# Order of small loads and head tiles, features-first queries and keys, scores in pairs, in a fused two-block transformer kernel

## What is computed

```python
mod = silu(c) @ w_ada + b_ada                     # 2048 x 12288, six vectors
h = rmsnorm(x, norm1_g) * (1 + sc1) + sh1
proj = h @ w_in                                   # 2048 x 5456
# stick-breaking: q_sb, k_sb, v_sb, 8 heads of 128; z = q k^T
# sparse attention: 8 heads of 128, one k and v, indexer of 16 heads of 64, top 64 keys
# then w_out, and a gated FFN with a causal conv of width 3
for l in range(2):                                # block 2, two layers
    proj = rms_norm(x) @ w_in[l]                  # 2048 x 6726
    # A: 6 heads of 128 with a forget gate, cum_logf = cumsum(log_sigmoid(a_f + b_forget))
    # B: latent attention, q = rms_norm(b_cq) @ w_uq (512 x 6*(128+64)), kv from w_ukv
    s = q_nope @ k_nope^T + q_rope @ k_rope^T     # 6 heads, 128 + 64 features, k_rope shared
    # C: differential attention, 4 heads, two score sets of 64 features each
    w = softmax(q1 @ k1^T) - lam * softmax(q2 @ k2^T)
    x = x + mixed @ w_out[l]
```

## Time and profile before

| | us |
|---|---|
| median of 3 runs (lowest, highest) | 2160.98 (2159.06, 2162.43) |
| profiled execution, own time | 2168.37 |
| its span | 2166.6 |
| PE busy | 2086.6 (96%) |
| PE weight loads busy | 1864.6 (86%) |
| DVE busy | 1405.5 (65%) |
| ACT busy | 1012.0 (47%) |
| POOL busy | 129.5 (6%) |
| chain that ended last, share of PE | 87% |

### The profile page before, as it was taken

One profiled execution on the slowest core, in us unless ns is written; L12 is line 12 of the kernel. 1 busy time (PEld: TensorE's weight loads), 2 busy tenths in 40 slices (PEclk: granted clock), 3 DMA queues, 4 the chain that ended last, 5 costly groups with the idle time before them and its releaser, 6 DMA issues.

```text
span 2166.6 us, 34209 instructions
## 1 busy us (share of the span) xinstructions
PE 2086.6 (96%) x13672; PEld 1864.6 (86%) x13672; DVE 1405.5 (65%) x2152; ACT 1012.0 (47%) x1498; POOL 129.5 (6%) x113
## 2 busy tenths in 40 slices
PE   4989999998999999999999999999999999999997
PEld 1668888787999999998888899998978999999876
DVE  2348998886667567666576576455566655565565
ACT  2324445635444454444545464444555544444453
POOL 0010000022000000000010111000001110000100
PEclk9999999999999999999999999999999999999999
DMA  9988798594777677656555456445545555545443
GB/s 352 382 314 316 237 385 312 209 343 140 231 236 231 204 247 256 193 162 242 191 179 203 160 173 200 160 151 166 164 160 182 173 152 175 190 156 162 169 175 117
DMA packets 267317, 462.96 MB, mean 214 GB/s; under 512 B 21526, under 2 KB 160028, under 8 KB 266652
## 3 DMA queue, kind: packets, MB, share of 16 engines
q1 hardware_dynamic: 265832, 459.66, 62.4%
q10 hardware_dynamic: 1332, 1.14, 0.2%
HBM read 458.62 MB, written 2.13 MB: 213 GB/s over the span
## 4 chain that ended last, share of the span: by engine, by line
PE 87%; DVE 6%; issue 2%; ACT 2%; DMA 1%; ACTq 1%; POOL 0%; SPq 0%; DVEq 0%; POOLq 0%
PE PS L312 40%; PE PS L311 18%; PE PS L1346 7%; PE PS L1347 7%; PE PS L1351 7%; PE PS L1189 2%; DVE WLO L302 2%; PE PS L413 1%; ACT WHI L294 1%; PE PS L1203 1%; ACTq L2280 1%; PE PS L1026 1%; DVE BIG L1673 1%; DMA SM<-b_forget 1%; DVE BIG L388 0%
## 5 line engine op out<-in xcount | busy, mean ns | idle before, releaser
L302 DVE TENSOR_TENSOR WLO<-RAWT,WHI 128x1024 fp32r<-128x1024 f32 (+6 forms) x694 | 829.3, 1201 | 404.9 <-ACT WHI L294 403.9
L294 ACT ACTIVATE WHI<-RAWT 128x1024 fp32r<-128x1024 f32 (+6 forms) x694 | 694.7, 1015 | 381.2 <-PE PS L1351 203.9
L312 PE MATMUL PS<-WHI,HH 128*128 128x512 f32 (+5 forms) x1432 | 561.5, 392 | 16.1 <-ACT WHI L294 7.2
L312 PE MATMUL PS<-WHI,HLO 128*128 128x512 f32 (+5 forms) x1432 | 549.5, 384 | 0.0
L312 PE MATMUL PS<-WLO,HH 128*128 128x512 f32 (+5 forms) x1432 | 374.7, 384 | 1.4 <-DVE WLO L302 1.4
L1346 PE MATMUL PS<-HH,WHI 128*128 128x256 f32 x1376 | 331.0, 281 | 9.4 <-POOL HLO L1045 5.8
L312 PEld LDWEIGHTS PS<-WHI,HH 128*128 128x128 f32 x1432 | 271.4, 190 | 73.2 <-DVE HLO L784 13.0
L1347 PE MATMUL PS<-HLO,WHI 128*128 128x256 f32 x1376 | 329.7, 280 | 0.0
L312 PEld LDWEIGHTS PS<-WLO,HH 128*128 128x128 f32 x1432 | 269.3, 189 | 49.1 <-DVE WLO L302 2.5
L312 PEld LDWEIGHTS PS<-WHI,HLO 128*128 128x128 f32 x1432 | 271.5, 190 | 44.4 <-issue 0.2
L1346 PEld LDWEIGHTS PS<-HH,WHI 128*128 128x128 f32 x1376 | 260.9, 190 | 11.1 <-POOL HLO L1045 7.2
(11 more groups left out here) (297 smaller groups left out, 1668.2 us busy)
## 6 DMA issues: line engine op xcount, KB each, us to landing
RAWT<-w_in SPq DMA_DIRECT2D x96, 1024.0 KB, 5.1
RAWT<-w_up SPq DMA_DIRECT2D x168, 512.0 KB, 4.8
AD<-w_ada SPq DMA_DIRECT2D x152, 512.0 KB, 6.1
RAWT<-w_out SPq DMA_DIRECT2D x96, 512.0 KB, 4.4
RAWT<-w_down SPq DMA_DIRECT2D x86, 512.0 KB, 4.6
BIG<-w_ada SPq DMA_DIRECT2D x40, 512.0 KB, 11.4
RAWT<-w_in SPq DMA_DIRECT2D x16, 832.0 KB, 4.5
RAWT<-w_in SPq DMA_DIRECT2D x16, 512.0 KB, 4.8
```

The source lines that it names most:

```text
L294: act.activation(WHI[:, (q % HL) * GR:(q % HL) * GR + size], r, ACT.Copy).then_inc(S("hi_done"), 1)
L302: dve.tensor_tensor(WLO[:, (q % HL) * GR:(q % HL) * GR + size], r, h.bitcast(F32), ALU.subtract)\
L312: pe.matmul(o, feat, weight, start=start, stop=stop)
```

## The change

Five edits.

1. *Small loads in two parts.* ACT issues 11 (constants, nine gain vectors, b_ada) first, then does its part of the norm, then issues the other 12 on a semaphore `set_late`. PE waits for the 11 and does two transposes. The other four transposes and the relative-bias product follow group 1 of stage 0, into banks 5 and 4; DVE's copies of them (`later_parameters`) come at the end of its stage 0. rel_table is stored a quarter later. PE's product for the lambdas moves from ahead of stage 1 to behind group 3 of stage 0, and waits there for rel_table's tile and for DVE.
2. *Order of the head.* prep(0), slices 13 to 15 and the columns come ahead of stage 0. In a stage, four slices of the next quarter follow each of groups 0 to 3, prep(2s + 2) stands ahead of the last four of them, the columns of the next quarter behind group 4. ACT and DVE interleave prep with WHI and WLO in a new order.
3. *Queries and keys features-first.* Pieces 5 to 8 get tt = 4; the eight turn jobs go.
4. *Scores in pairs.* Latent and difference jobs are computed two at a time, at the even job's group, product by product in turn; the odd job writes bank 7. The forget gate's products move to bank 6 and 6 groups earlier, with a wait of PE at group 50 for their copy.
5. *Rotary columns in one piece.* The second latent piece holds 2 nope tiles only, each tile in a bank of its own; the third holds all 384 rotary columns rows-first.

```diff
-            lat = [Piece(l, None, w_uq_2[l], nope[0:4], 4, 0, "q", 4), Piece(l, None, w_uq_2[l], nope[4:] + rot[0:4], 4, 4, "q", 2, 0),
-                   Piece(l, None, w_uq_2[l], rot[4:], 4, None, "q", 0, 256)] + \
+            lat = [Piece(l, None, w_uq_2[l], nope[0:4], 4, 0, "q", 4), Piece(l, None, w_uq_2[l], nope[4:], 4, 4, "q", 2, 0),
+                   Piece(l, None, w_uq_2[l], rot, 4, None, "q", 0, 0)] + \
...
-        first_pieces = [Piece(0, k, w_in[0], cols, 16, None, "first")
+        first_pieces = [Piece(0, k, w_in[0], cols, 16, None, "first", 4 if 5 <= k <= 8 else 0)
...
+            def scores(job, m):
+                return PS[:, 7 if job.get("paired") and m % 2 else banks[0], :]
             def pe_scores(i):
                 job, m, b = each(i)
+                if job.get("paired") and m % 2:
+                    return
                 ge(eng, S("sm_lg"), 2 * m)
+                both = jobs[i:i + 2] if job.get("paired") else [job]
                 for hf in range(2):
-                    prs = job["qk"](hf)
-                    for z, (l, r) in enumerate(prs):
-                        mm = eng.matmul(blk(bank(0), hf), l, r, start=z == 0, stop=z == len(prs) - 1)
-                mm.then_inc(S("sm_s"), 1)
+                    prs = [j["qk"](hf) for j in both]
+                    for z in range(len(prs[0])):
+                        for k, (l, r) in enumerate([pr[z] for pr in prs]):
+                            mm = eng.matmul(blk(scores(both[k], m + k), hf), l, r, start=z == 0, stop=z == len(prs[0]) - 1)
+                mm.then_inc(S("sm_s"), len(both))
...
-        TURN_AT = [30, 31, 32, 33, 34, 48, 49, 50, 51, 52, 54, 55, 66, 67, 73, 74, 80, 81]
+        TURN_AT = [30, 31, 32, 33, 34, 48, 49, 50, 51, 52]
...
             if pe:
-                at(45, steps[0])
-                at(48, steps[1])
+                at(39, steps[0])
+                at(42, steps[1])
+                at(50, lambda: eng.wait_ge(S("cum_tmp"), l + 1))
             elif act:
-                at(43, steps[0])
-                at(51, steps[1])
+                at(35, steps[0])
+                at(45, steps[1])
             else:
-                at(42, lambda: (evicted(eng, x[3]), steps[0]()))
-                at(45, steps[1])
-                at(48, steps[2])
+                at(33, lambda: (evicted(eng, x[3]), steps[0]()))
+                at(37, steps[1])
+                at(42, steps[2])
```

The head on PE:

```diff
+            prep(pe, 0)
+            for kt in range(13, KT):
+                ada_matvec(pe, 0, kt)
+            ada_columns(pe, 0)
             for s in range(4):
-                prep(pe, 2 * s)
-                for kt in range(13, KT):
-                    ada_matvec(pe, s, kt)
-                ada_columns(pe, s)
                 prep(pe, 2 * s + 1)
-                if s < 3:
-                    ada_matvec(pe, s + 1, 0)
                 for i in range(6):
                     head_pe(pe, 6 * s + i)
-                    if s < 3:
-                        for kt in beside[i]:
+                    if s == 0 and i == 1:
+                        later_parameters()
+                    if s == 0 and i == 3:
+                        pe.wait_ge(S("rel_t"), 1)
+                        pe.wait_ge(S("lam_row"), 1)
+                        pe.wait_ge(S("h_dve"), 2)
+                        pe.matmul(PS[:, 6, 480:482], ones[0:1, :], TR0[0:1, 28:30], start=True, stop=True)\
+                          .then_inc(S("lam_mm"), 1)
+                        pe.wait_ge(S("lam_out"), 1)
+                    if s < 3 and i < 4:
+                        if i == 3:
+                            prep(pe, 2 * s + 2)
+                        for kt in range(4 * i, 4 * i + 4):
                             ada_matvec(pe, s + 1, kt)
+                    if s < 3 and i == 4:
+                        ada_columns(pe, s + 1)
```

The head on DVE (ACT in the same way with `head_hi`):

```diff
+                for q in range(6 * s, 6 * s + 2):
+                    head_lo(dve, q)
...
+                for z in range(2):
+                    prep(dve, 2 * s + z)
+                    head_lo(dve, 6 * s + 2 + z)
+                if s == 0:
+                    later_parameters()
```

More of the change, by code:

```diff
@@ L543, in first_out @@
             act.wait_ge(S("mm_done"), count)
[L544 to L545 removed]
+            for m in range(2):
+                bank, o = PS[:, 2 * (pc.cn % 2 if pc.cn > 2 else pc.cn) + m, :], 0
                 for i, (c0, n) in enumerate(pc.cols):
[L547 to L548 removed]
+                    if pc.tt:
+                        op = act.activation(tiles(B1, c0 + 2 * m * P, P, 2),
+                                            bank.rearrange("p (j h x) -> p j h x", j=2, h=2), ACT.Copy)
+                    else:
+                        op = act.activation(B1[:, m, c0:c0 + n], bank[:, o:o + n], ACT.Copy)
                     o += n
[L550 removed]
+                op.then_inc(S("ev_act" if m == 0 else "ev_dve"), 1)
         def head_out(act, c):
@@ L638, in piece_pe @@
                         w = slice(o + t * P, o + (t + 1) * P)
-                        parts.append((t // 2, PS[:, 2 * b + t // 2, (t % 2) * T:(t % 2 + 1) * T], hh[:, kt, :], hl[:, kt, :],
-                                      WHI[:, w], WLO[:, w], True))
+                        bank, c = (t, 0) if n == 2 * P else (t // 2, t % 2 * T)
+                        parts.append((bank, PS[:, 2 * b + bank, c:c + T], hh[:, kt, :], hl[:, kt, :], WHI[:, w], WLO[:, w], True))
                     o, m = o + pc.tt * P, n - pc.tt * P
@@ L688, in bank_out @@
                 return bank, tiles2(col, per, t + 2 * m, 2)
+            if pc.tt == 2 and not n:
+                return bank[:, 0:T].rearrange("p (h x) -> p h x", h=2), QN[:, pc.dst + m]
             if 2 * m < pc.tt:
@@ L1230, in dve_logits @@
                 for hf in range(2):
-                    eng.tensor_tensor_reduce(blk(LG[b], hf), blk(bank(0), hf), job["mask"](hf, b),
+                    eng.tensor_tensor_reduce(blk(LG[b], hf), blk(scores(job, m), hf), job["mask"](hf, b),
                                              -job["scale"], 3e38, ALU.add, ALU.min,
@@ L1970, in mla_jobs @@
             return [dict(qk=qk(i), mask=lambda hf, b: right(CST[:, C_CHNK:C_CHNK + T], hf), scale=BSC,
-                         v=lambda kb, i=i: b2(kb, KVB + 768 + i * P), put=tiles2(BCQ, 3, i), form="turned") for i in range(6)]
+                         v=lambda kb, i=i: b2(kb, KVB + 768 + i * P), put=tiles2(BCQ, 3, i), form="turned",
+                         paired=True) for i in range(6)]
         def diff_jobs(l):
@@ L1980, in diff_jobs @@
                                v=lambda kb, i=i: b2(kb, CV + i * P), put=B2[:, :, CQ + i * P:CQ + (i + 1) * P],
-                               form=("first", "second")[s])
+                               form=("first", "second")[s], paired=True)
                     if s:
@@ L2277, in _ @@
                 o += n
-            act.dma_start(rows[0:2 * FT, 1, :], conv_b[0].rearrange("(r x) -> r x", x=P)).then_inc(S("set_in"), 16)
+            act.dma_start(rows[0:96, 5, :], b_ada[0].rearrange("(r x) -> r x", x=P)).then_inc(S("set_in"), 16)
+            act.wait_ge(S("x_in"), 32)
+            prep_norm(act, "act", ty, chain)
+            with nc.allow_non_contiguous_dma(reason="256 positions"):
+                act.dma_start(TR0[:, 16:18].bitcast(I32), positions.rearrange("a (h p) -> p (a h)", p=P))\
+                  .then_inc(S("set_late"), 16)
@@ L2288, in _ @@
             act.dma_start(BFG, b_forget_2.rearrange("l n -> (l n)").rearrange("(a n) -> a n", a=1)
-                         .broadcast_to((P, 12))).then_inc(S("set_in"), 16)
-            act.wait_ge(S("x_in"), 32)
-            prep_norm(act, "act", ty, chain)
+                         .broadcast_to((P, 12))).then_inc(S("set_late"), 16)
             prep = prep_w_in("act", ty)
             for s in range(4):
-                ready = 6 * s + (2 if s == 3 else 4)
-                for q in range(6 * s, ready):
+                for q in range(max(6 * s - 2, 0), 6 * s + 2):
@@ L2396, in _ @@
             for s in range(4):
[L2397 to L2399 removed]
+                for q in range(max(6 * s - 2, 0), 6 * s):
+                    head_lo(dve, q)
                 if s == 1:
@@ L2402, in _ @@
                     lambdas()
+                for q in range(6 * s, 6 * s + 2):
+                    head_lo(dve, q)
+                if s == 1:
                     dve.wait_ge(S("lam_mm"), 1)
                     dve.tensor_copy(NLAM, PS[:, 6, 480:482]).then_inc(S("lam_out"), 1)
-                ready = 6 * s + (2 if s == 3 else 3)
-                for q in range(6 * s, ready):
-                    head_lo(dve, q)
                 ada_rows(dve, s)
```

119 lines of the change are left out of this document (51 added, 68 removed).

## The result

The changed kernel takes 2136.18 us (median of 4 runs, 2132.61 to 2138.97); before was at 2161.7 in the same comparison. The ratio is 0.9877 with an interval of 0.9861 to 0.9892: **25.5 us saved**, where 28.5 were forecast. 2132.5 was predicted and the range of 2123 to 2148 holds the result. The profiled execution took 2138.03 us (span 2136.2), 30.3 less than the profiled one of before.

A forecast was written before the change was run, and what follows sets the result against it. PE was taken to bound nearly everywhere, except the largely DMA-bound head and DVE's stretch at 200 to 335 us. 9.9 + 1.6 + 14.1 + 2.9 = 28.5 us off 2168.4 profiled gives 2139.9, median 2132.5; range 2123 to 2148.

The forecast's parts named there:

- Head, forecast 9.9 us: Head, 0 to 146 us: last stage starts at 137.2 against 145.85 (8.6), clock gap gone (2.3), group 1 waits (1.0 lost).
- 74.2 + 1.8 + 2.9 + 4.1 = 83.0: Head, stage 1: the slice landing at 74.2 us plus the work behind it puts the stage's start at 83.0.
- The stage starts at 52: Head, stage 0: ACT free at 44.0 us and DVE at the columns about 47.5, so the start stays at 52.
- the sentence on the first wait: Head: removing PE's 12.5 us wait for the small loads brings no gain from the first wait itself.
- Queries and keys, forecast 1.6: Stick-breaking queries and keys: six transposes that count save 2.6 us, features-first groups give 1.0 back; bounds +2.4 to -3.5.
- 13 x 0.075 = 1.0 comes back: Queries and keys: 13 features-first groups paced by PE each take 0.075 us longer, 1.0 us in all.
- Pairs, forecast 14.1: Scores: latent pair 2.58 instead of 3.78 us (7.2 saved), difference pair 0.85 instead of 1.70 (6.8); bounds 0 to -16.
- Rival 1: Scores: the pairs don't overlap, only halved changes of form count, 9 us less saved: 2141.5; chance 0.10.
- Rotary columns, forecast 2.9: Latent queries: 12.7 us instead of 14.13, 1.43 in each of 2 layers; bounds 0 to -3.
- Rival 2: Head: paced by DMA or by the lambda chain, it ends where it did: 2142.4; chance 0.12.
- Rival 3: Head: late issues block ACT, deciding from a mean of 4.1 us an issue; slower, 2181; chance 0.03.
- Rival 4: Forget gate: its moved sums stall PE in both layers, 3 us each: 2138.5; chance 0.05.

The follow-up runs named there:

- serial difference pair: Changed kernel with pairs kept in one slot and two banks, but one job's products all before the other's: 2144.66 us, ratio 0.9916.
- the order of form: Changed kernel with each latent pair's four nope products first, then its four rope products: 2131.70 us, ratio 0.9844.
- repetition: The changed kernel itself, unchanged, measured again on one chip with a later candidate: 2134.39 us, ratio 0.9883.
- rows-first kernel: Changed kernel with the stick-breaking queries and keys rows-first and their eight transpose jobs back: 2140.7 us, ratio 0.9894.

## Why the prediction was right

**Head, forecast 9.9 us, measured 7.1 to 9.7 at the mark behind it, 8.2 in the mean and 7.6 in the changed kernel's own profile.** Of the later stages, each is within 0.8 us: 83.0 forecast and 82.26 measured, 110.4 and 110.18, 137.2 and 137.66. The wait for the landing of w_ada slices was the right bound for stage 2. For stage 1 the nearness is luck. The forecast had four slices left behind a landing at 74.2 ("74.2 + 1.8 + 2.9 + 4.1 = 83.0"); PE takes the last slice at about 73, and without the clock dip at 73 us the stage starts at 80.32 to 80.49. Stage 2 hardly follows it (109.63 to 109.81 there). The clock dip comes behind PE's wait of 2.1 us for the lambdas, which the prediction took for free. The wait alone is: all nine profiles with this order on PE have it, five of them without a dip. That the dip ahead of stage 3 would go is shown; stages 1 and 2 of before had one each as well, of which the sum said nothing. Group 1's wait was put at 1 us and was 1.02.

The step that failed is stage 0: "The stage starts at 52". It started at 47.76. I had ACT free at 44.0 with three conv_w issues of 4.4 us, and the last slice landing where it had landed before, at 44.6. ACT was free at 39.65, and the slice came some 3 us earlier (PE's wait for it ends at 41.47), because SP can load a slot only when PE's product has freed it, and the 12.5 us wait stood in front of those products. In size the sentence on the first wait was wrong by 4 us for stage 0. In effect it was right, as the run with the small loads first shows: from stage 2 on nothing of it is left that can be told from the 0.6 us between profiles.

**Queries and keys, forecast 1.6, measured 1.9 to 3.0.** The six transposes are there. The mis-sized term is "13 x 0.075 = 1.0 comes back": the price was read from the earlier trace rows, where two groups took 5.65. Those two stand right behind score products, as the 5.65 of the changed kernel at 1485.15 do; the three groups at 1491.78, which do not, take 8.18, 2.73 each. The 0.2 us belong to the place behind the scores, once, and not to every group. Here the group takes 5.46 / 2 = 2.73, rows-first 5.51 / 2 = 2.755, so nothing comes back. The Trainium skill's overhead of some 60 cycles a matmul ("TensorEngine Tiling (Array Packing)", Instruction Overhead), read as added to each, is not borne out by these rows either.

**Pairs, forecast 14.1, measured 15.1.** Latent pair 2.58 forecast, 2.56 measured; difference pair 0.85 and 0.86. Rival 1 is refuted by every row, and side-by-side work is shown by the serial difference pair, in which the second job costs 0.01. What was left out of the sum: around a difference pair some 0.1 us more goes than the score lines themselves show (four pairs save 3.8, not 3.4). That the latent pair came within 0.02 has luck in it: the order of form puts one entry and exit at 0.39, not 0.3, and with that the sum 1.32 + 0.66 + 2 x 0.39 would have given 2.76. Some other term of it is too large by 0.2, and no run shows which.

**Rotary columns, forecast 2.9, measured 2.7.** 12.78 us against 12.7.

**Rivals 2 to 4.** Rival 2, the head held by DMA, is half true: the last stages are at the DMA bound and it came out where the forecast put it, not where they started before. Rival 3 fell: 12 issues took 15.4 us, 1.3 each, where it needed 4.1. Yet they are on the chain of stage 0: ACT rounds its first tile at 39.70, and DVE copies the sums only behind two WLO tiles, at 43.04, some 0.5 us after PE's last product (42.55). Beside rival 3 stood the Trainium skill's rule that each DMA engine takes packets from the queues in turn ("DMA: Bandwidth & Descriptors", Queues, rings and completion order). The trace does not settle it: most late issues took 0.3 us with SP's queue full, but one of lambda_q took 7.27. Of rival 2's other half, the lambda chain, PE's wait of 2.1 us is there and holds nothing up by itself. Rival 4 did not show: no wait of PE names the forget sums.

**From the ledger to the median.** The forecast's profiled time was 2139.9 and it was 2138.03. The 7.4 us between before's profiled execution and its median were carried over to the changed kernel; its own profiled execution stood 1.85 above its median. That step was 5.5 us too large; the profiled time, 1.9 below its forecast, made part of it good, and 3.7 us are left, by which 2132.5 missed. The distance was no property of the kernel: over 11 runs beside the experiments before had medians of 2163.2, 2166.5 and 2162.6.

## What to carry to other kernels

The longest wait of an engine need not be worth anything. Before removing it, ask what the next resource is, here a DMA queue at 390 GB/s, and put the same question to one's own improvements: a load or a tile is late not for its reader alone but for all that stands behind the reader. Products that use half of the rows should stand next to products of the other half with nothing between them, and all products of one form together; alternating them one by one adds nothing where they already follow each other. And a profiled execution's distance to the median must not be carried from one kernel to the next.

## What the runs showed that was not expected

**Two paces.** Features-first products of the same line come at two paces that hold for 80 us and more. They change at the pause of PE in the middle of w_up (4 us up to 720.83 in the changed kernel), and once without one. Windows of w_up, in the changed kernel and in its repetition:

```profile
607.00:627.00 20.00, 20.00 (x179) 20.00 (x178) 15.57 (x19) 9.58 (x12) 1.02 (x1) 1.00 0.72 235
767.00:787.00 20.00, 20.00 (x172) 20.00 (x171) 14.84 (x19) 9.72 (x12) 1.02 (x1) 1.00 0.74 235
```

```profile
607.00:627.00 20.00, 20.00 (x179) 20.00 (x179) 14.89 (x19) 8.96 (x11) 1.02 (x1) 1.00 0.73 235
767.00:787.00 20.00, 20.00 (x179) 20.00 (x178) 15.29 (x19) 9.10 (x11) 1.02 (x1) 1.00 0.71 230
```

20 / 179 = 0.112 us a product, or 20 / 172 = 0.116, at full clock and with WHI and WLO ready. In the changed kernel's profile the second half of w_up ran at the slower pace and its first products span 487.6 to 983.9, in the repetition 486.8 to 976.7: 6.4 us. Of the eleven other profiles, before included, four have one slow half. Besides, every profile has the slower pace from 885 to 905 us on to the end of w_up; the change comes there with no pause, in before's profile and in the repetition's right behind 16 small products of the w_ada sums (L397). A slow half is of the size by which single runs of one kernel differ; that it is their cause is not shown, since only profiled executions tell the pace. What chooses the pace is open.

**The clock in the first 50 us.** It differs from profile to profile of the same program. In the changed kernel's it is 1.00 over 20 to 50 us, in its repetition's 0.50. In the rows-first kernel's windows too PE had the lower level (1.2 GHz) nearly throughout:

```profile
20.00:50.00 30.00, 17.34 (x105) 6.03 (x106) 9.79 (x25) 8.96 (x10) 1.28 (x1) 0.50 1.06 373
```

Stage 0 starts at 47.76, 47.48 and 47.87 in the three all the same: what it waits for there is landings and ACT's issues, not PE's pace.

**Free partners.** Two fp32 products over 64 rows each, in opposite halves and different banks, take the time of one (0.86 us for a difference pair, 0.85 for a single job). I had expected it as likely; that it needs no alternation I had not.
